# Attention heads taken in pairs on row and column halves of TensorE, with four buffers each

## The reference

```
# A: window_attention
s_win = einsum('bnqhgd,bnkhd->bnhgqk', qb, kb) * scale     # |q - k| <= 128, else NEG_INF
s_ctx = einsum('bnqhgd,bkhd->bnhgqk', qb, k_c) * scale
p = softmax(concatenate([s_win, s_ctx, s_sink]))
o = einsum(p[window], v_l) + einsum(p[ctx], v_c)
# D: dense_gqa
s = einsum('bqhgd,bkhd->bhgqk', qg, k) * d ** -0.5
p = softmax(s);  o = einsum('bhgqk,bkhd->bqhgd', p, v)
```

## Time and profile before

| | |
|---|---|
| median of 3 runs | 2142.07 us (2141.47 to 2149.24) |
| the profiled execution | 2148.33 us, of which its span is 2146.5 us |
| TensorE, VectorE, ScalarE busy | 1657.4, 905.9, 569.5 us |
| attention of layer 0 and layer 1 | 70.6 and 49.7 us |

### The profile page before, as it was taken

How to read it: one execution, slowest core, us unless ns; L and a number is a source line. 1 busy time by engine, 2 the same in 40 slices (tenths; PEclk the granted TensorE clock), 3 DMA queues, 4 the chain that set the end, 5 groups by cost and what they waited for, 6 DMA issues and landing times. The chain is left out here.

```text
span 2146.5 us, 39607 instructions
## 1 busy us (share of the span) xinstructions
PE 1657.4 (77%) x11491; PEld 714.8 (33%) x11492; DVE 905.9 (42%) x3060; ACT 569.5 (27%) x1173; POOL 347.5 (16%) x357
## 2 busy tenths in 40 slices
PE   3999799858878888888886499698556656766675
PEld 2545554422223223322322455454212211212221
DVE  2245563364444444444446336543522322322334
ACT  2142352212322333333231214242111211221221
POOL 0001300002222222222220001210011111111110
PEclk8999799989999999999999699789888888988888
DMA  8315510447999899998837823813499989999974
GB/s 272 130 70 193 190 60 1 176 172 285 376 373 412 342 375 365 405 365 333 346 114 313 273 80 118 334 32 147 174 361 364 412 344 414 409 401 356 407 300 181
DMA packets 165603, 578.28 MB, mean 269 GB/s; under 512 B 24956, under 2 KB 29792, under 8 KB 148648
## 3 DMA queue, kind: packets, MB, share of 16 engines
q1 hardware_dynamic: 134592, 515.49, 61.9%
q0 software_dynamic: 24256, 60.03, 7.5%
q10 hardware_dynamic: 6696, 1.98, 0.4%
HBM read 557.87 MB, written 37.89 MB: 278 GB/s over the span
## 5 line engine op out<-in xcount | busy, mean ns | idle before, releaser
L1225 PE MATMUL bank<-arena 128*32 128x512 f32 x4160 | 544.1, 645 | 291.6 <-DMA arena<-in_exp_w_up 171.1
L1225 PEld LDWEIGHTS bank<-arena 128*32 128x32 f32 x4160 | 118.0, 115 | 494.8 <-issue 312.6
L692 POOL DMA_INDIRECT yrows<-arena x128 | 130.1, 1016 | 915.4 <-ACT arena L925 915.4
L1250 PE MATMUL bank<-arena 128*32 128x512 f32 x2048 | 247.0, 598 | 18.3 <-issue 16.5
L1735 DVE TENSOR_TENSOR arena<-arena,bank 64x512 f32<-64x512 f32 x130 | 88.4, 680 | 353.0 <-ACT arena L907 353.0
L920 ACT ACTIVATE arena<-bank 128x128 f32<-128x128 f32 x128 | 35.5, 278 | 685.6 <-PE bank L1281 685.6
L673 POOL DMA_INDIRECT arena<-hrows,arena x134 | 137.2, 1024 | 149.5 <-DVE arena L1709 108.5
L1693 DVE COPY arena<-arena 128x12 bf16 (+1 forms) x272 | 63.6, 234 | 193.4 <-issue 193.4
L991 PE MATMUL bank<-arena 128*128 128x512 f32 (+3 forms) x384 | 131.6, 504 | 11.7 <-DVE arena L1391 11.7
L1215 PEld LDWEIGHTS bank<-arena 128*128 128x128 f32 x528 | 73.8, 209 | 110.6 <-issue 110.6
L994 PE MATMUL bank<-arena 128*128 128x512 f32 (+1 forms) x256 | 100.0, 552 | 0.0
(11 more groups left out here) (304 smaller groups left out, 1910.2 us busy)
## 6 DMA issues: line engine op xcount, KB each, us to landing
arena<-in_exp_w_gate SPq DMA_DIRECT2D x128, 1024.0 KB
arena<-in_exp_w_up SPq DMA_DIRECT2D x128, 1024.0 KB
arena<-in_exp_w_down SPq DMA_DIRECT2D x128, 1024.0 KB
arena<-in_w_ada SPq DMA_DIRECT2D x10, 3072.0 KB
arena<-yrows SPq DMA_DIRECT2D x24, 1024.0 KB, 16.2
arena<-in_w_ada SPq DMA_DIRECT2D x8, 2048.0 KB
arena<-in_w_in SPq DMA_DIRECT2D x8, 2048.0 KB
arena<-in_w_out SPq DMA_DIRECT2D x4, 2048.0 KB
```

The costliest lines, as they stand in the source:

```text
L692: pool.indirect_dma_start(out=yrows, out_offset=bass.IndirectOffsetOnAxis(ap=SIXS[u], axis=0), in_=YSB[u], in_offset=None, bounds_check=2 ...
L1225: ins = pe.matmul(bank[0][r:r + UNIT, :], XGT[:, c, un, hh, :], wv[un][:, :, hh, c, :], start=(c == 0), stop=(c == 3))
L1250: ins = pe.matmul(bank[2][r:r + UNIT, :], HIDT[:, c, UNIT * un:UNIT * un + UNIT], wv[un][:, c, cg * 512:(cg + 1) * 512], start=(c == 0), s ...
```

## The change

The heads of a query tile are listed as 0, 3, 1, 2, and two neighbours form a pair; heads 0 and 3, and heads 1 and 2, lie on different row halves (scores) and on different column halves (values). `scores`, `turn` and `values` take a pair: the two score matmuls stand back to back ahead of both masks, and the value matmuls of the two heads alternate. Score banks, buffers PB and buffers PTB become four each (bank 7 is added, and PTB moves to where the LRU's inputs were); the banks of the transposes stay two. TensorE's order per pair p becomes: transposes of p, scores of p + 2, values of p - 1. VectorE does four bounds and two scalings first, and then for each p: scalings of pair p + 1, bounds of pair p + 2. ScalarE: both copies of p, both exponentials of p + 2. The parameter edit comes after pair 4's step.

```
@@ buffers
-        PB = [at(rPROJ + 5152 + 512 * k, 512) for k in range(3)]
-        PTB = [at(rPROJ + 5152 + 1536 + 512 * k, 512) for k in range(2)]
+        PB = [at(rPROJ + 5152 + 512 * k, 512) for k in range(4)]
+        PTB = [at(rPROJ + 7200 + 512 * k, 512) for k in range(4)]
-        score_bank = (0, 1, 6)
+        score_bank = (0, 1, 6, 7)
-          units = [... for h in range(4)]
+          units = [... for h in (0, 3, 1, 2)]
@@ ScalarE
+                exps(0)
+                exps(1)
+                for p in range(NPAIR):
+                    for u in (2 * p, 2 * p + 1):
+                        nk = keys_of(units[u][1])
+                        act.wait_ge(pe_pt, u + 1)
+                        if u >= 4:
+                            act.wait_ge(pe_pv, u - 3)
+                        act.activation(PTB[u % 4][:, 0:nk], bank[2 + u % 2][:, 0:nk], ACT.Copy).then_inc(a_pt, 1)
+                    if p + 2 < NPAIR:
+                        exps(p + 2)
@@ TensorE
+                def scores(p):
+                    for u in (2 * p, 2 * p + 1):
+                        g, t, h = units[u]
+                        nk = keys_of(t)
+                        r = slice(64 * (h // 2), 64 * (h // 2) + 64)
+                        if u >= 4:
+                            pe.wait_ge(a_ex, u - 3)
+                        sb = bank[score_bank[u % 4]]
+                        masked = g == "A" and t >= 2
+                        ins = pe.matmul(sb[:, 0:nk], QT[g][r, h % 2, tile_of(t)], QT[g][r, 2, 0:nk], start=True, stop=not masked)
+                        if not masked:
+                            ins.then_inc(pe_s, 1)
+                    g, t, h = units[2 * p]
+                    if g == "A" and t >= 2:
+                        for u in (2 * p, 2 * p + 1):
+                            ...
+                            pe.matmul(o, IDB, NEGU if t == 2 else NEGL, start=False, stop=True).then_inc(pe_s, 1)
+                def turn(p):
+                    for u in (2 * p, 2 * p + 1):
+                        nk = keys_of(units[u][1])
+                        pe.wait_ge(v_p, u + 1)
+                        if u >= 2:
+                            pe.wait_ge(a_pt, u - 1)
+                        for kb in range(nk // P):
+                            ins = pe.transpose(bank[2 + u % 2][:, tile_of(kb)], PB[u % 4][:, tile_of(kb)], IDENT)
+                        ins.then_inc(pe_pt, 1)
+                def values(p):
+                    j = p // 2
+                    pe.wait_ge(a_pt, 2 * p + 2)
+                    if j >= 2 and p % 2 == 0:
+                        pe.wait_ge(v_ot, j - 1)
+                    nkb = keys_of(units[2 * p][1]) // P
+                    for kb in range(nkb):
+                        for u in (2 * p, 2 * p + 1):
+                            g, t, h = units[u]
+                            o = bank[4 + j % 2][64 * (h % 2):64 * (h % 2) + 64, (h // 2) * P:(h // 2 + 1) * P]
+                            ins = pe.matmul(o, QKV[g][:, kb, 384 + 64 * (h // 2):448 + 64 * (h // 2)], PTB[u % 4][:, tile_of(kb)],
+                                            start=(kb == 0), stop=(kb == nkb - 1))
+                            if kb == nkb - 1:
+                                ins.then_inc(pe_pv, 1)
+                scores(0)
+                scores(1)
+                for p in range(NPAIR):
+                    turn(p)
+                    if p + 2 < NPAIR:
+                        scores(p + 2)
+                    if p >= 1:
+                        values(p - 1)
+                values(NPAIR - 1)
@@ VectorE
+                for u in range(4):
+                    bound(u)
+                scaled(0)
+                scaled(1)
+                for p in range(NPAIR):
+                    if p + 1 < NPAIR:
+                        scaled(2 * p + 2)
+                        scaled(2 * p + 3)
+                    if p + 2 < NPAIR:
+                        bound(2 * p + 4)
+                        bound(2 * p + 5)
+                    if p == 4:
+                        ...
+                    if p >= 3 and p % 2 == 1:
+                        heads_out(p // 2 - 1)
```

More of the change, by code:

```diff
@@ L193, in build @@
         NCUM = at(o + 48, 32)
-        SCOL = at(o + 224, 3, 4)
-        MX = at(o + 236, 3, 4)
+        SCOL = at(o + 224, 4, 4)
+        MX = at(o + 240, 4, 4)
         CT2 = CT
@@ L487, in build @@
           NTOK = T - K0
-          units = [(g, t, h) for g in "AD" for t in ((2, 3) if last else (2, 3, 0, 1)) for h in range(4)]
+          units = [(g, t, h) for g in "AD" for t in ((2, 3) if last else (2, 3, 0, 1)) for h in (0, 3, 1, 2)]
           NU = len(units)
+          NPAIR = NU // 2
           done_of = [(pe_piece, n + 1) for n in range(N_ADA1)] + [(pe_pj, 4 * k) for k in range(1, 6)]
@@ L852, in _, with exps @@
                     act.activation(QT["AD"[j // 3]][:, j % 3, q0:], bank[4 + j % 4][:, q0:], ACT.Copy).then_inc(a_qk, 1)
-                for u in range(NU + 2):
-                    if u < NU:
+                def exps(p):
+                    for u in (2 * p, 2 * p + 1):
                         g, t, h = units[u]
-                        q = u % 3
+                        q = u % 4
                         nk = keys_of(t)
                         act.wait_ge(v_nm, u + 1)
-                        if u >= 3:
-                            act.wait_ge(pe_pt, u - 2)
+                        if u >= 4:
+                            act.wait_ge(pe_pt, u - 3)
                         act.activation(PB[q][:, 0:nk], bank[score_bank[q]][:, 0:nk], ACT.Exp, bias=SCOL[:, q, 1:2], scale=HD ** -0.5,
@@ L1090, in _ @@
                 pe.wait_ge(a_ym, 2)
[L1092 to L1125, removed]
+                def scores(p):
[3 more added lines that the diff above has]
+                        r = slice(64 * (h // 2), 64 * (h // 2) + 64)
+                        if u >= 4:
+                            pe.wait_ge(a_ex, u - 3)
[7 more added lines that the diff above has]
+                        for u in (2 * p, 2 * p + 1):
+                            sb = bank[score_bank[u % 4]]
+                            o = sb[:, 384:512] if t == 2 else sb[:, 256:384]
+                            pe.matmul(o, IDB, NEGU if t == 2 else NEGL, start=False, stop=True).then_inc(pe_s, 1)
```

4 lines of the change are left out of this document (1 added, 3 removed).

## The result

The changed kernel takes 2108.28 us (median of 4 runs, 2106.28 to 2109.38); the kernel before took 2143.94 us beside it (2141.47 to 2149.24). The ratio is 0.983 with a 95% interval of 0.981 to 0.985: 35.7 us, or 1.7%, faster. Forecast were 2110.6 us and 31.5 us.

A forecast was written before the change was run, and what follows sets the result against it. TensorE was taken to bound attention. Attention sums of 52.6 against 70.6 us (layer 0) and 36.2 against 49.7 (layer 1) save 18.0 and 13.5, together 31.5: median 2142.07 to 2110.6 us, range 2101 to 2126.

The forecast's parts named there:

- The overlaps: TensorE in attention: two heads stream in the time of one; scores 2.10 to 1.05 us (D), values 2.04 to 1.03.
- transposes stay: TensorE's transposes per pair keep their cost: 1.08 us in A, 1.18 in D, 0.72 with 256 keys.
- VectorE per pair: Attention: VectorE's work, half an output copy and a 0.2 us wait exceed TensorE's time, setting the pair period.
- half output copy: VectorE in attention: 0.2 us per pair added to the work of two units.
- Filling, layer 0: Start of layer 0's attention: first transposes after 5.5 us, next pairs' transposes 2.6 and 2.8 us later.
- the slower rival: TensorE in attention kept at 1.2 GHz by short gaps: +14 to +20 us, time about 2158; chance 0.03.
- Filling, layer 1: Start of layer 1's attention at 1.2 GHz, 2.4 from about 13 us on: pair 2 begins at 15.4 us.
- The signs: Attention traces: head scores starting within 0.01 us, 16 values in about 1.05 us; clock under 1.00 in layer 0 refutes.
- All that follows moves up: After attention, out-projection and expert weight loads start earlier: each microsecond saved counts as one of the total.
- a): Attention on TensorE: scores do not overlap, values do; some 16 us saved, time 2126; chance 0.09.
- b): Attention: handover between engines costs 0.5 us more per pair over 24 pairs; saved 19, time 2123; chance 0.12.
- c): Attention on TensorE: no overlap at all, filling longer by a microsecond each; time 2142 to 2144; chance 0.04.

The follow-up runs named there:

- e7: Kernel before with two more transposes per unit on TensorE, 96 in all: 2145.9 us, ratio 1.003 to the kernel before.
- e5: Kernel before with one more VectorE operation per unit, 48 in all: 2149.3 us, ratio 1.004 to the kernel before.
- e8: Changed kernel with VectorE starting bounds 0, 1, scalings 0, 1, bounds 2, 3: 2104.67 us, ratio 0.983 to the kernel before.
- e1: Changed kernel with heads listed 0, 1, 2, 3, so only the values of a pair can overlap: 2127.77 us, ratio 0.993.
- e3: Changed kernel with heads listed 0, 1, 2, 3 and values one head after the other: 2135.28 us, ratio 0.997.
- e10: Changed kernel with heads listed 0, 1, 2, 3 and VectorE's first two scalings made before bounds 2 and 3: median 2126.41 us, ratio 0.992.
- e2: Changed kernel with heads listed 0, 2, 1, 3 and values one head after the other, so only scores can overlap: 2115.09 us, ratio 0.989.
- e6: Changed kernel with two more transposes per unit on TensorE, 96 in all: 2107.4 us, ratio 0.984 to the kernel before.
- e9: Changed kernel with VectorE's scalings and bounds in turn, also at the start: 2113.51 us, ratio 0.985 to the kernel before.
- e11: e8 plus two full float32 matmuls ahead of layer 1's scores: median 2110.56 us, ratio 0.984 to the kernel before.
- e12: Changed kernel with VectorE's scalings and bounds in turn and two full matmuls ahead of layer 1's scores: 2111.61 us, ratio 0.984.

## Why the prediction was right

Point by point, by its own steps.

- **The bound.** TensorE set the pace of attention: e7 shows it (9.2 of 10.5 us), and e5 that VectorE did not.
- **The overlaps.** Carried over from lines 1030 and 1052, they held at 512 columns. TensorE per pair was forecast at 3.3 (A) and 3.25 (D), measured 3.11 in D. The step "transposes stay" missed 0.15: they take 1.03 for two heads in a row.
- **VectorE per pair.** A 3.85 forecast, 3.68 measured; D 3.4 against 3.07 to 3.36; with 256 keys 3.0 against 2.65 to 3.02 (A) and 2.5 against 1.81 to 2.71 (D). In A the work was right (3.46 forecast, 3.43 measured) and the wait was 0.25 where I took 0.2; too large was the half output copy of 0.2, since no copy falls into that pair. In D I left out that starts overlap by 0.08 after a long operation, which I took off for 256 keys only.
- **Filling, layer 0.** First transposes after 5.65 us (forecast 5.5), but the next two pairs 3.4 and 4.1 later, not 2.6 and 2.8. About half of these 2 us is the clock's dip, which I didn't foresee: the scores of pair 2 ran at 1.2 GHz, and VectorE waited 1.24 us for them. The rest was a count too short: in e8, without a dip, pair 2 still started 12.1 us after the first scores, where I had 10.9. I had put a fall of the clock only into the slower rival, as a matter of the steady pairs, where it never fell. The dip came behind 3 us in which TensorE idled during the filling, which my own sum contained.
- **Filling, layer 1.** 14.1 us to pair 2 (forecast 15.4): the clock rose earlier, as the bound "an earlier rise would add 1 to 3 us" allowed.
- **The sums.** 52.6 and 36.2 forecast, 51.9 and 34.3 measured. In layer 0 the filling took 2.2 us more than forecast, the pairs behind it 3.0 less and the tail 0.2 more: that the sum is right within 0.7 is luck. The gain was 4 us larger than forecast by the medians, 2.6 by attention.
- **The signs.** Score records of two heads start 0.006 us apart and 16 value records take 1.02 us, as the prediction asked. But it also said that a granted clock under 1.00 in layer 0's attention would make the forecast wrong. The clock was 0.97 there and the forecast held: the sign was set too sharp, as a dip of 3.4 us costs little where VectorE sets the pace.
- **"All that follows moves up".** It did: 34.1 us in attention, 35.7 in the runs.
- **The rule on transposes.** By the Trainium skill, page "TensorE: Matmul & The Clock Gate", section "Part 4: PE-mode transpose", transposes don't bring the full clock. The trace of before had shown the clock rising over transposes alone, and the changed kernel with its larger share of them kept 1.00 in every steady stretch. The rival built on it did not come. Where the clock did fall in the change, TensorE had idled for 3.0 us (layer 0) and 2.6 us (layer 1) shortly before.
- **The rule on PSUM.** By the Trainium skill, page "TensorEngine Tiling (Array Packing)", section "PSUM Bottleneck", tiling speeds up TensorE but not the emptying of PSUM. TensorE's 89% and VectorE's 93% in the steady stretch agree with it in part: VectorE became the limit in A, but of its 3.68 us only the two row maxima, 0.69 and 0.68, read PSUM; the scalings work in SBUF.
- **The rivals' prices.** For a), no overlap of the scores, I gave some 16 us of gain; e1 gained 14. That agreement is luck: at 2.4 GHz a pair of D took 3.96 in place of my 4.3, and the clock took the rest back. For b), a dearer handover, the wait was 0.25 and not 0.2 plus 0.5. For c), no overlap at all, I gave no gain; e3 gained 6.6 us in spite of 44 us at 1.2 GHz, because I priced grouping at nothing. Its price was wrong by the 0.87 us per pair that e3 shows, 0.49 from grouping and 0.38 from values that overlap after all.

## What to carry to other kernels

Before packing small matmuls onto halves of the array, look for a place in the same trace where two halves already alternate, and count starts, not durations; then add up the engine that comes next, for it will set the pace (here 14.0 us of extra VectorE work went from costing 2.6 us to costing 12.2). Price the grouping too: doing transposes, scores and values for two heads at a time saved 0.15 to 0.2 us each. And when the change makes the filling longer, look at what TensorE's clock does there: behind some 3 us of idle time came 3.4 us at 1.2 GHz here (e8, without them, is half a microsecond shorter in that layer) and 20 us in e1. And hold a profile against the times of the other runs before you reason from it: e10's is of a run 12 us faster than the median.

## What the hardware showed that I had not expected

- TensorE stayed at 1.2 GHz for 20.4 us while 100% busy (e1, layer 0) and for 27 us while some 90% busy (e1 and e3, layer 1), both with float32 scores on one row half at a time.
- TensorE's work up to the first transposes of layer 1 is the same in the change, e2 and e6 but for which heads are paired. Its clock rose 3.3 us after the first scores in the change and in e2, and 12.0 us after them in e6. Other orders on VectorE gave 9.7 us (e8) and 16.0 (e9), one row half at a time 9.8 (e10), 13 (before) and 27 (e1, e3). No run shows what decides between them. Only with two matmuls of 128 rows and 512 columns ahead of the scores was the clock up before them, in both kernels that had these (e11 and e12).
- Matmuls of the second head began while those of the first, ahead of them in the program and on the other column half, were still to come. In e3 the 16 value records take 1.51 us against 1.89 on one half; the second head's first record starts at 1424.69 and the first head's last one at 1425.01.
